# Causal logits of two heads as 64-row matmuls into two PSUM banks, and the forget bias as one 64-row matmul

## The reference, cut to what matters

```python
logf = log_sigmoid(f_logit + b_f)                      # one number per token and head
c = cumsum(logf, axis=1)
logits = einsum("bqhd,bkhd->bhqk", q, k) * scale       # d = 64, per block of 128 queries, keys up to its end
logits = logits + c[:, :, s0:s1, None] - c[:, :, None, :s1]
...
sc = einsum('bqhmd,bkhmd->bhmqk', q_blk, k) * scale    # second block: 4 heads x 2 maps, d = 64
sc = sc - slopes * dist
```

## Time and profile before

| | us |
|---|---|
| median of 3 runs (lowest, highest) | 1049.44 (1048.48, 1049.68) |
| span of the profiled execution, first to last instruction | 1046.5 |
| PE busy | 1022.3 (98%) |
| DVE busy | 651.0 (62%) |
| ACT busy | 493.6 (47%) |
| POOL busy | 115.3 (11%) |
| mean granted TensorE clock (1 is full) | 0.994 |

### The profile page before, as it was taken

How to read it: one execution, slowest core, us unless ns; L and a number is a source line. 1 busy time by engine, 2 the same in 40 slices (tenths; PEclk the granted TensorE clock), 3 DMA queues, 4 the chain that set the end, 5 groups by cost and what they waited for, 6 DMA issues and landing times.

```text
span 1046.5 us, 19409 instructions
## 1 busy us (share of the span) xinstructions
PE 1022.3 (98%) x8282; PEld 1007.0 (96%) x8282; DVE 651.0 (62%) x616; ACT 493.6 (47%) x625; POOL 115.3 (11%) x91
## 2 busy tenths in 40 slices
PE   8999999998999999989999999999999999999997
PEld 7998999998999999979999999999999999999996
DVE  6655767958655555595555557775684475555554
ACT  5443445645433434554343434655755564343433
POOL 5000000566000000450000002000030020000000
PEclk9999999999999999999999999999999999999999
DMA  8653364453545565545646464633444345555531
GB/s 277 206 163 120 121 242 162 134 188 122 200 162 200 164 198 168 182 137 198 197 164 200 160 200 162 200 123 122 162 161 147 116 161 168 194 171 190 183 138 41
DMA packets 138107, 175.39 MB, mean 168 GB/s; under 512 B 3940, under 2 KB 122950, under 8 KB 137926
## 3 DMA queue, kind: packets, MB, share of 16 engines
q1 hardware_dynamic: 136006, 171.24, 49.7%
q10 hardware_dynamic: 2048, 3.38, 0.9%
HBM read 173.56 MB, written 1.05 MB: 167 GB/s over the span
## 4 chain that ended last, share of the span: by engine, by line
PE 88%; DVE 7%; issue 2%; ACT 1%; POOL 1%; DMA 1%; SPq 0%; DVEq 0%; ACTq 0%; POOLq 0%
PE bank L373 27%; PE bank L374 27%; PE bank L375 27%; DVE act_lo L1437 3%; DVE w_lo L1424 1%; PE bank L457 1%; DVE x_T L1539 1%; PE bank L821 1%; PE bank L842 1%; DMA stage<-in_w_in 1%; ACT w_hi L899 1%; PE bank L460 0%; PE bank L600 0%; DVE w_lo L1561 0%; PE bank L616 0%
## 5 line engine op out<-in xcount | busy, mean ns | idle before, releaser
L373 PE MATMUL bank<-act_hi,w_hi 128*128 128x256 f32 x1648 | 471.8, 286 | 12.7 <-DVE act_lo L1437 9.2
L374 PE MATMUL bank<-act_lo,w_hi 128*128 128x256 f32 x1648 | 467.5, 284 | 0.0
L375 PE MATMUL bank<-act_hi,w_lo 128*128 128x256 f32 x1648 | 467.4, 284 | 0.0
L373 PEld LDWEIGHTS bank<-act_hi,w_hi 128*128 128x128 f32 x1648 | 317.3, 193 | 18.1 <-DVE act_lo L1437 7.6
L374 PEld LDWEIGHTS bank<-act_lo,w_hi 128*128 128x128 f32 x1648 | 317.6, 193 | 0.1
L375 PEld LDWEIGHTS bank<-act_hi,w_lo 128*128 128x128 f32 x1648 | 317.4, 193 | 0.0
L1430 DVE TENSOR_TENSOR w_lo<-stage,w_hi 128x2048 fp32r<-128x2048 f32 x81 | 185.6, 2292 | 141.3 <-ACT w_hi L906 141.3
L1424 DVE TENSOR_TENSOR w_lo<-stage,w_hi 128x2048 fp32r<-128x2048 f32 x79 | 183.9, 2333 | 90.1 <-ACT w_hi L899 89.7
L899 ACT ACTIVATE w_hi<-stage 128x2048 fp32r<-128x2048 f32 x79 | 150.7, 1910 | 72.9 <-PE bank L375 71.0
L906 ACT ACTIVATE w_hi<-stage 128x2048 fp32r<-128x2048 f32 x81 | 154.0, 1902 | 54.8 <-PE bank L375 54.8
L373 PE MATMUL bank<-ffn_hi,w_hi 128*128 128x256 f32 x480 | 135.9, 283 | 0.0
(11 more groups left out here) (300 smaller groups left out, 1233.9 us busy)
## 6 DMA issues: line engine op xcount, KB each, us to landing
stage<-in_ffn_w SPq DMA_DIRECT2D x66, 1024.0 KB, 5.1
stage<-in_w_in SPq DMA_DIRECT2D x33, 1024.0 KB, 5.2
stage<-in_w_gate_up SPq DMA_DIRECT2D x22, 1024.0 KB, 5.1
stage<-in_w_down SPq DMA_DIRECT2D x11, 1024.0 KB, 4.8
stage<-in_w_out SPq DMA_DIRECT2D x8, 1024.0 KB, 4.9
stage<-in_mem_w_kv SPq DMA_DIRECT2D x8, 1024.0 KB, 5.3
stage<-in_w_branch SPq DMA_DIRECT2D x4, 1024.0 KB, 5.4
stage<-in_mem_w_q SPq DMA_DIRECT2D x4, 1024.0 KB, 4.9
```

The lines of the kernel that those rows point to most:

```text
L373: pe.matmul(dst, w, x, start=first, stop=False, skip_group_check=not group)
L374: pe.matmul(dst, w, lo_x, start=False, stop=False, skip_group_check=not group)
L375: return pe.matmul(dst, lo_w, x, start=False, stop=last, skip_group_check=not group)
```

## The change: what it does

- `q_pad` is no longer padded: one copy `q_T` holds both heads, even in partitions 0 to 63, odd in 64 to 127. `query` and `diff_query` write it with one instruction of 128 partitions each; both clears on POOL go, and those of `logf` and `fe`.
- `logits(g)` now takes two head pairs, b and b + 1, and is called for g = 0, 2 and 4, 6. For each pair j it issues the matmul of rows 0 to 63 (the even head) into bank ACC + b and that of rows 64 to 127 (the odd head) into bank ACC + b + 1, one after the other. Then the bias, again for rows 0 to 63 and 64 to 127: one matmul where there were two.
- For that, minus the cumulative sum must lie in partitions 0 to 31 (rounded) and 32 to 63 (rest), and the same in 64 to 127. The forget gate's 8 weight columns, the bias `b_f` and the selector are repeated at partitions 0, 32, 64 and 96; the small elementwise steps work on 128 partitions where they had 8; `b_f` takes four small DMAs on SP's queue for one, and the selector table four DMAs of 32 partitions on ACT's queue for one of 128.

```diff
-                    pe.wait_ge(lg_free, first + g - 3)
-                for par_ in range(2):
-                    dst = pair[ACC + b][:, par_, 0:nk]
-                    mm = pe.matmul(dst, q_pad[:, par_, b, qt * P:qt * P + P], k_T[:, b, 0:nk],
-                                   start=True, stop=not bias)
+                    pe.wait_ge(lg_free, first + g - 2)
+                for j in (b, b + 1):
+                    for i in range(2):
+                        own = slice(64 * i, 64 * i + 64)
+                        mm = pe.matmul(pair[ACC + b + i][:, j - b, 0:nk], q_T[own, j, qt * P:qt * P + P],
+                                       k_T[own, j, 0:nk], start=True, stop=not bias)
                     if bias:
-                        pe.matmul(dst, sel_r[:, 2 * b + par_, :], negc_hi[:, 0:nk], start=False, stop=False)
-                        mm = pe.matmul(dst, sel_r[:, 2 * b + par_, :], negc_lo[:, 0:nk], start=False, stop=True)
-                mm.then_inc(lg_done, 1)
+                        for i in range(2):
+                            own = slice(64 * i, 64 * i + 64)
+                            mm = pe.matmul(pair[ACC + b + i][:, j - b, 0:nk], sel_r[own, 2 * j + i, :],
+                                           negc[own, 0:nk], start=False, stop=True)
+                mm.then_inc(lg_done, 2)
...
-            for g in range(4):
+            for g in (0, 2):
                 logits(g, 0, True)
...
-            pe.matmul(bank[AUX][0:8, T:2 * T], logf_tok[:, 0, :], tri, start=True, stop=False)
+            pe.matmul(bank[AUX][:, T:2 * T], logf_tok[:, 0, :], tri, start=True, stop=False)
...
-            act.dma_start(sel, a["consts"][:, C_END:C_END + 1024].rearrange("p (h m) -> p h m", h=8)
-                          ).then_inc(table_landed, 16)
+            for r in range(0, P, 32):
+                act.dma_start(sel[r:r + 32, :, :], a["consts"][0:32, C_END:C_END + 1024].rearrange("p (h m) -> p h m", h=8)
+                              ).then_inc(table_landed, 16)
...
-                dve.scalar_tensor_tensor(q_pad[0:64, 0, b:b + 2, :], src[0:64, :, :], 0.125, over(rs, p=slice(0, 64)),
-                                         ALU.mult, ALU.mult)
-                dve.scalar_tensor_tensor(q_pad[64:P, 1, b:b + 2, :], src[64:P, :, :], 0.125, over(rs, p=slice(64, P)),
-                                         ALU.mult, ALU.mult).then_inc(up_free, 1)
+                dve.scalar_tensor_tensor(q_T[:, b:b + 2, :], src, 0.125, over(rs), ALU.mult, ALU.mult).then_inc(up_free, 1)
...
-            dve.scalar_tensor_tensor(negc_lo, bank[AUX][0:8, T:2 * T], -1.0, negc_hi.bitcast(F32), ALU.mult, ALU.subtract
-                                     ).then_inc(aux_free, 1)
+            for r in (slice(32, 64), slice(96, P)):
+                ins = dve.scalar_tensor_tensor(negc[r], bank[AUX][r, T:2 * T], -1.0, negc[r].bitcast(F32),
+                                               ALU.mult, ALU.subtract)
+            ins.then_inc(aux_free, 1)
```

More of the change, by code:

```diff
@@ L164, in build @@
         gain_rows = table[:, 0:4, :].rearrange("p a b -> p (a b)")
-        sel_r = mix_hi[0:8, 4:8, :].rearrange("p a b -> p (a b)").rearrange("p (h m) -> p h m", h=8)
-        negc_hi, negc_lo = mix_lo[0:8, 4, :], mix_lo[0:8, 5, :]
+        sel_r = mix_hi[:, 4:8, :].rearrange("p a b -> p (a b)").rearrange("p (h m) -> p h m", h=8)
+        negc = mix_lo[:, 4, :]
+        q_T = q_pad[:, 0, :, :]
+        wf_hi4, wf_lo4 = (w.rearrange("p k (g n) -> p k g n", g=4)[:, :, :, 0:8] for w in (wf_hi, wf_lo))
+        wf4 = wf[:, :, None, :].to_broadcast([P, KD, 4, 8])
         alibi, decay = table[:, 0:4, :], table[:, 4:8, :]
@@ L284, in parameters @@
                 rows(r, 1, a[name], 64, at)
-            rows(BF, 1, a["b_f"], 8, 0)
+            for at in range(0, P, 32):
+                rows(BF, 1, a["b_f"], 8, at)
         def store(engine, t, j):
@@ L584, in _ @@
             pe.wait_ge(x_done, 4)
-            for g in range(4):
+            for g in (0, 2):
                 logits(g, 0, True)
             up(HC + 1, act_hi, act_lo)
-            for g in range(4, 8):
+            for g in (4, 6):
                 logits(g, 0, True)
@@ L710, in _ @@
             wait_read(pe, DQ + 1)
-            for g in range(4):
-                if g % 2 == 0:
-                    pe.wait_ge(aux_free, A_DK[g // 2] + 1)
+            for g in (0, 2):
+                pe.wait_ge(aux_free, A_DK[g // 2] + 1)
                 logits(g, 8, False)
             up(RQ, act_hi, act_lo)
-            for g in range(4, 8):
+            for g in (4, 6):
                 logits(g, 8, False)
@@ L1029, in _ @@
             act.wait_ge(wf_landed, 16)
[L1030 to L1031 removed]
+            act.wait_ge(zeroed, 6)
+            act.activation(wf_hi4, wf4, copy).then_inc(wf_hi_done, 1)
             warm(ACT.Sqrt)
@@ L1045, in _ @@
             act.wait_ge(fz_done, 1)
-            act.activation(fe[0:8, :], fe[0:8, :], table_exp).then_inc(fexp_done, 1)
+            act.activation(fe, fe, table_exp).then_inc(fexp_done, 1)
             act.wait_ge(fexp_done, 1)
-            act.activation(fe[0:8, :], fe[0:8, :], ACT.Ln, bias=1.0).then_inc(fln_done, 1)
+            act.activation(fe, fe, ACT.Ln, bias=1.0).then_inc(fln_done, 1)
             hi(8)
             scaled_tok(V + 1, [v_tok[:, t, 256:512] for t in range(2)], tok)
-            act.wait_ge(table_landed, 16)
-            act.activation(sel_r, sel[0:8, :, :], copy)
+            act.wait_ge(table_landed, 64)
+            act.activation(sel_r, sel, copy)
             hi(9)
@@ L1056, in _ @@
             act.wait_ge(aux_done, A_CUM + 1)
-            act.activation(negc_hi, bank[AUX][0:8, T:2 * T], copy, scale=-1.0).then_inc(negc_done, 1)
+            act.activation(negc, bank[AUX][:, T:2 * T], copy, scale=-1.0).then_inc(negc_done, 1)
             hi(12)
@@ L1201, in diff_query @@
                 if j == 0:
[L1202 to L1205, removed]
+                    act.wait_ge(mem_lo_done, 8)
+                    act.wait_ge(sq_done, 2)
+                act.activation(q_T[:, 2 * j:2 * j + 2, :], src, copy, scale=par[:, DQN:DQN + 1]).then_inc(up_free_act, 1)
             def diff_key_squares(j):
@@ L1477, in read_scores @@
                     m = 2 * b + i
-                    src = pair[ACC + b][:, i, 0:nk]
+                    src = pair[ACC + b - b % 2 + i][:, b % 2, 0:nk]
                     if first == 0:
```

35 lines of the change are left out of this document (14 added, 21 removed).

## The result

After the change: 1033.54 us, median of 4 runs (1033.36 to 1034.78), against 1049.56 before (1048.48 to 1051.79, 4 runs). The ratio is 0.9848 [0.9835, 0.9860], so the change saves 16.0 us. The sign and the place of the gain were right; its size was not.

What follows compares the result with a forecast made beforehand. PE (TensorE), busy 98% of the span, was taken to bound the kernel. Savings of 3.25 + 5.4 + 0.6 + 1.55 + 0.3 = 11.1 us gave a span of 1035.4, plus 2.9 to the median: 1038.3 us, range 1036.0 to 1042.6.

Steps and rivals of the forecast that it cites:

- A: First block, tile 0's logits with bias on PE: window of 6.15 us to become 2.9, saving 3.25 us.
- B: First block, tile 1's logits with bias on PE: window of 8.34 us to become 2.95, saving 5.4 us.
- C: Second block, tile 0's logits without bias on PE: window of 1.82 us to become 2.1, losing 0.3 us.
- First, loads: Inside the logits groups: each entry pays a full weight load of 0.105 us; 0.63 us a pair with bias, 0.42 without.
- Loads of the two halves go side by side: Rival, logits groups: weight loads of both halves overlap, A falls by 1.25 us and C by 0.8; 1036.3, chance 0.1.
- Second, streams: Inside the logits groups: two halves stream at once, a pair taking 0.64 us in B and 0.43 in D.
- D: Second block, tile 1's logits without bias on PE: window of 3.45 us to become 2.1, saving 1.35 us.
- What is late next: Transposes behind D: PE waits about 0.45 us for DVE, so C and D together save 0.6 us.
- The clock: Chunk HC + 1 behind A: the drop to the lower clock level disappears, saving 1.55 us.
- The start: Ahead of chunk 2, DVE's `query` loses one instruction: saves 0.3 us; ACT's four table DMAs, 1.7 us together, stay hidden.
- in turn: Rival, logits groups: the two halves work one after the other, saving 8.1 us in all; 1041.3, chance 0.2.
- standing at each change of halves: Rival, inside the logits groups: every change between halves stands 0.2 us, making the kernel slower; 1052.6, chance 0.05.

Runs made afterwards that it cites:

- the kernel with a bias of 128 rows: Kernel after, but queries padded as before and bias one matmul of 128 rows, selector zero in rows that don't count, no halves: 1039.21 us, ratio 0.9903.
- the kernel with one half for all: Kernel after, but odd heads computed from the even heads' rows, so all 64-row matmuls use rows 0 to 63: 1039.42 us, ratio 0.9906.
- The experiment with the exchanged loops: Kernel after with two loops exchanged, so within a call both even heads come first, then both odd heads: 1034.40 us, ratio 0.9862.
- the one with 64-row biases: The padded-query kernel with one bias matmul of 128 rows, but that bias matmul has 64 rows: 1045.05 us, ratio 0.9961.
- the second-block kernel: Kernel before, with only the second block's logits done by halves from unpadded queries: 1048.66 us, ratio 0.9994.
- half by half over a tile: Kernel after, with one call for four head pairs, four even heads then four odd, bank waits per tile: 1039.77 us, ratio 0.9904.
- bias twice: Kernel after, with each bias matmul issued two times: 1035.59 us in one run.
- the last: Kernel after with first-block values split by output columns, and the second block's tile 1 put ahead of tile 0: 1031.57 us, ratio 0.9824.

## Why the prediction was too small

**What bounds the kernel** held: 14.3 of the 14.6 us are PE's busy time. **The standing time at a change of rows** held as well: 0.40 us a head by the forecast's halves of 0.20, and 0.40 before, held against the kernel with a bias of 128 rows; with 64 rows it is 0.34 in A and 0.39 in B. The size was right and its place misread: the second entry of line 457 starts at 86.33 and not at 86.23 (in B at 100.20, not 100.09), 0.21 us behind the first where two entries inside C are 0.11 apart. So of the 0.46 us in A 0.11 stand behind the head's first entry, 0.10 ahead of line 460, 0.11 between the two bias matmuls (86.54 to 86.70, for a stream of 0.05) and 0.15 on the way back. **One edge per group** was forecast at 0.4 and measured at 0.34 to 0.40.

**The step that failed is "First, loads".** It let every entry pay a full load of 0.105 us, one after the other for the two halves: 0.63 us a pair with bias, 0.42 without. Measured are 0.335 and 0.22, about half of it. The loads of the two halves go side by side as the matmuls do. The Trainium skill, page "TensorEngine Tiling (Array Packing)", Key Properties, has this too: different tiles load and multiply in parallel, and the trace agrees (sixteen loads in 0.97 us). I had weighed against it the section LDWEIGHTS of the Trainium skill, page "TensorE: Matmul & The Clock Gate", on the load's cost by columns. For each half by itself that holds: the loads of one half start 0.11 us apart in A, as those of 128 rows do in the padded kernel. This is the rival "Loads of the two halves go side by side", which I had given a chance of 0.1 at 1036.3. It makes A 1.2 us shorter than forecast and C 0.8. The nearest row had no way of showing it, since all its loads have 128 rows; I took its value as if the nearest row were also the likeliest. The prediction priced the halving at 1.25 + 0.8 us, and the kernel with one half for all, held against after, shows the factor of two in all four groups (eight slots for four). By itself this step would have moved the forecast only to 1036.3, inside the range; the rest of the miss is in the sum below.

**"Second, streams"** was right in kind and too slow in B. Two halves at once was the better end, but I let the order of issue cost a third slot of 0.213 a pair, 0.64 us. Measured is 0.55, which is 0.43 of float32 and 0.12 of bias: the halves keep step, and there is no third slot. The experiment with the exchanged loops shows that a start does not wait for its neighbour's later entries. B became 2.59 for 2.95. In D, without bias, two slots of 0.215 a pair were right to 0.03 us.

**A, once more.** The forecast saved 3.25 from a window of 6.15 (rows 5, which ends 0.14 early), and the group went to 1.68 for 2.9. Together A, B and C make 4.61 - 3.25 + 5.85 - 5.4 + 0.5 + 0.3 = 2.6 us of the missing gain.

**What is late next** was right: a wait for DVE at `turn_probs`, forecast 0.45 and shown as 0.60. From D to the end of the program 0.74 us are given back. C's unforeseen gain is what made it larger: PE comes earlier by 0.5 + 1.33 = 1.83 us in place of 1.05, and of that 1.83 - 0.74 = 1.1 are left. The forecast had 0.6.

**The clock** behind A: forecast 1.55, measured 1.45, and the window behind A reads 1.00. The kernel with a bias of 128 rows, without a change of rows, has the drop gone too, and the one with 64-row biases has it back. I had not seen that this drop differs from run to run (1.4 or 2.9 us), nor a second one: before, PE waits 2.1 us for POOL near 215 us and then runs at a lower clock. Windows of before, PE, around it:

```profile
217.00:221.00 4.00, 3.42 (x16) 0.63 0.74 251
```

After has a wait of the same kind, 1.85 us at 205.12, and no lower clock behind it. Between B and C this is worth 1.4 us, and nothing ties it to the change: of the experiments' traces the 128-row kernel, the second-block kernel, half by half over a tile, bias twice and the last have this drop, the others do not. What decides it stays open. For this reason differences of 1 to 2 us between medians are read here with their windows.

**The start**: 0.3 forecast and 0.25 found ahead of A, but it is luck that they agree; three things make up the 0.25. At chunk 2 the time from PE's transpose to the chunk's second matmul fell from 0.66 us (28.05 to 28.71) to 0.22 (28.41 to 28.63): 0.44 won, the forecast's 0.3 and a little more. The cumulative sum, counted as nothing, gave 0.17: before, its last entries have 8 weight columns and the chunk starts 0.31 us behind them (73.53 to 73.84); after, with 128, it starts 0.14 us behind (73.46 to 73.60). Against these stands a third stretch of the lower clock, during chunk 0. Windows of after, PE:

```profile
13.00:17.00 4.00, 3.47 (x15) 0.50 1.08 309
17.00:20.00 3.00, 3.00 (x17) 0.53 0.63 185
```

Before, the two windows read 0.57 and 1.00. The longer stretch made PE 0.36 us late by the transpose (28.41 for 28.05). It too differs from run to run: the kernel with one half for all, with the same instructions up to there, reads 1.00 in both.

ACT's four DMAs were guessed short. Its queue and first work after, for the earlier trace rows:

```profile
2.76 3.10 ACTq L1022 DMA_DIRECT2D table<-in_consts  x4
...
7.63 0.91 ACT L921 ACTIVATE act_hi<-x_T,first_gain 128x256 fp32r<-128x256 f32 x2 [0.24 <-DVE x_T L1563]
```

3.10 us for the 1.7 that I took; of the 1.69 us in which ACT waited, 0.24 are left. It stayed hidden, by a quarter of a microsecond.

**The sum.** To the span of 1035.4 the forecast added 2.9 us, the distance from the profiled span to the median. Every execution's time here is 1.8 us above its span (1033.68 against 1031.9). The other 1.1 us were the profiled execution being one of the faster ones of before: of 16 executions of before on record, the five with a mean granted clock of 0.994 or more, as the profiled one had, took 1048.1 to 1048.9 us, the others 1048.8 to 1050.2. That the slower ones had the dearer drop behind A, which after has not to pay, fits but isn't shown, since only the profiled execution has a trace. So 1038.3 - 1.1 (this) - 2.6 (A, B, C) - 1.4 (clock near 217) + 0.3 (the wait behind D) + 0.1 (HC + 1) + 0.05 (the start) gives 1033.65 for a profiled 1033.7.

**The other rivals** fell: in turn (1041.3), since the kernel with one half for all is that case, and its slots are those of a single head where after has a pair in them; standing at each change of halves, since no row inside a group has it; the clock behind another group, since all five windows read 1.00.

## What to carry to other kernels

- On this chip a few small matmuls of another row count between large ones cost 0.34 to 0.40 us for each pair of changes, far more than their streams, and the lower clock can follow them (1.4 to 2.9 us here). Give them the neighbours' row count, with zeros if need be (here, with two bias matmuls made one, 9.1 of 14.6 us), or gather them so that the count changes once.
- Then put matmuls of 64 rows (or of 64 output columns) in alternation between the halves: a pair costs what one costs, loads included. Alternate in the order of issue; two heads in a row of one half still come near it (1.06 us more in the four groups), four in a row do not (4.2).
- After PE is faster, look at who hands it the next data: exchanging the order of two tiles took back the 0.6 us that the change had lost to VectorE. A cost that no row shows deserves more chance at its far end than 0.1.

## What the runs showed that I had not expected

- Loads of 64 rows for the two halves go side by side: sixteen in 0.97 us.
- A 64-row matmul alone is no faster than one of 128 rows (slots of 0.335, 0.55, 0.22 and 0.43 us in both kernels).
- A matmul for the idle half goes out ahead of earlier ones for the busy half, over a reach of three to four entries (inferred from the pace).
- 128 to 64 rows and back stands nearly as long as 128 to 8 rows: 0.34 and 0.39 us against 0.40.
- The lower clock comes or stays away in traces of the same instructions, during chunk 0, behind A and near 217 us, and moves the time by 0.4 to 1.5 us each time.
- Two heads in the two column halves of one bank run at once (0.70 us for two; the stage 2.95 for 5.23). Whether two row halves may share a bank wasn't tried.
